# When the top-k rounds of an attention layer run on VectorE: one tile's rounds spread over other score units

## The reference

```python
s_h = jnp.einsum('bthd,bsd->bths', qib, ki)
s_idx = jnp.einsum('bths,bth->bts', jax.nn.relu(s_h), wib)
s_idx = jnp.where(causal[None], s_idx, -jnp.inf)
_, sel = lax.top_k(s_idx, topk)              # topk = 128 of at most 512 keys
...
logits = jnp.where(valid[:, None], logits, -jnp.inf)
p = jax.nn.softmax(logits, axis=-1)
return jnp.einsum('bhtk,btkhd->bthd', p, vg.astype(jnp.float32))
```

## Time and profile before

| | us |
|---|---|
| median of 3 runs | 781.57 |
| lowest, highest | 778.15, 786.66 |
| profiled execution, whole | 778.69 |
| its span, first to last instruction | 776.9 |
| TensorE busy (matmul) | 715.9 |
| VectorE busy | 462.6 |
| ScalarE busy | 338.2 |
| GpSimd busy | 265.9 |
| mean granted TensorE clock, share of full speed | 0.974 |

### The profile page before, as it was taken

How to read it: one execution, slowest core, us unless ns; L and a number is a source line. 1 busy time by engine, 2 the same in 40 slices (tenths; PEclk the granted TensorE clock), 3 DMA queues, 4 the chain that set the end, 5 groups by cost and what they waited for, 6 DMA issues and landing times.

```text
span 776.9 us, 9937 instructions
## 1 busy us (share of the span) xinstructions
PE 715.9 (92%) x3584; PEld 569.2 (73%) x3584; DVE 462.6 (60%) x831; ACT 338.2 (44%) x508; POOL 265.9 (34%) x209
## 2 busy tenths in 40 slices
PE   0898999999788879889799999999999999999998
PEld 0786877787574546678698888888878887888886
DVE  4858788886899787878553665764455445000005
ACT  3534246836522644532366455554544554111110
POOL 2003798409902200000022444344334434433440
PEclk9989999999979989899989999999999999999999
DMA  8941231160274643773811313322331332232202
GB/s 305 384 122 37 101 105 58 68 188 17 30 76 72 199 155 110 270 271 108 298 55 31 128 60 106 108 84 78 108 108 61 102 108 87 76 109 109 85 23 108
DMA packets 63017, 91.46 MB, mean 118 GB/s; under 512 B 11947, under 2 KB 41411, under 8 KB 62916
## 3 DMA queue, kind: packets, MB, share of 16 engines
q1 hardware_dynamic: 59456, 89.44, 35.8%
q10 hardware_dynamic: 3523, 1.54, 0.7%
HBM read 86.28 MB, written 4.69 MB: 117 GB/s over the span
## 4 chain that ended last, share of the span: by engine, by line
PE 80%; DVE 11%; ACT 5%; issue 3%; DMA 1%; ACTq 0%; SPq 0%; DVEq 0%
PE bank L1577 23%; PE bank L1579 23%; PE bank L1578 23%; PE bank L1582 3%; PE bank L1608 1%; DVE arena L1286 1%; PE bank L1920 1%; DVE stat L1283 1%; DMA xh<-in_x 1%; PE bank L1587 1%; PE bank L1808 1%; DVE arena L1151 1%; DVE stat L1070 1%; PE bank L1915 1%; PE bank L1788 1%
## 5 line engine op out<-in xcount | busy, mean ns | idle before, releaser
L482 POOL TENSOR_TENSOR w_lo<-w_raw,w_hi 128x2048 fp32r<-128x2048 f32 x34 | 156.8, 4612 | 387.0 <-ACT w_hi L676 192.8
L1577 PE MATMUL bank<-act_hi,w_hi 128*128 128x512 f32 (+2 forms) x384 | 148.1, 386 | 4.8 <-DVE act_lo L1514 3.2
L1578 PE MATMUL bank<-act_lo,w_hi 128*128 128x512 f32 (+2 forms) x384 | 146.9, 383 | 0.0
L1579 PE MATMUL bank<-act_hi,w_lo 128*128 128x512 f32 (+2 forms) x384 | 146.8, 382 | 0.0
L1577 PE MATMUL bank<-w_hi,act_hi 128*128 128x512 f32 x240 | 101.2, 422 | 2.1 <-DVE act_lo L1180 2.1
L1578 PE MATMUL bank<-w_lo,act_hi 128*128 128x512 f32 x240 | 96.8, 403 | 0.0
L1579 PE MATMUL bank<-w_hi,act_lo 128*128 128x512 f32 x240 | 96.7, 403 | 0.0
L676 ACT ACTIVATE w_hi<-w_raw 128x2048 fp32r<-128x2048 f32 x26 | 49.7, 1913 | 88.0 <-PE bank L1579 87.4
L1577 PEld LDWEIGHTS bank<-act_hi,w_hi 128*128 128x128 f32 x384 | 73.2, 191 | 19.8 <-issue 3.9
L1578 PEld LDWEIGHTS bank<-act_lo,w_hi 128*128 128x128 f32 x384 | 73.3, 191 | 14.3 <-issue 0.2
L1579 PEld LDWEIGHTS bank<-act_hi,w_lo 128*128 128x128 f32 x384 | 73.2, 191 | 14.3
(11 more groups left out here) (303 smaller groups left out, 1192.9 us busy)
## 6 DMA issues: line engine op xcount, KB each, us to landing
w_raw<-in_w_up SPq DMA_DIRECT2D x44, 512.0 KB, 4.5
arena<-in_w_ada SPq DMA_DIRECT2D x6, 2048.0 KB, 15.3
w_raw<-in_w_down SPq DMA_DIRECT2D x22, 512.0 KB, 4.1
w_raw<-in_w_in SPq DMA_DIRECT2D x10, 1024.0 KB, 5.0
arena<-in_w_ada SPq DMA_DIRECT2D x8, 1024.0 KB, 6.5
xh<-in_x SPq DMA_DIRECT2D x8, 512.0 KB, 8.4
w_raw<-in_w_out SPq DMA_DIRECT2D x4, 1024.0 KB, 12.5
s_mem<-in_w_ada SPq DMA_DIRECT2D x4, 1024.0 KB, 7.1
```

The lines of the kernel that those rows point to most:

```text
L482: nc.gpsimd.tensor_tensor(w_lo[:, slot, 0:width], w_raw[:, slot, 0:width], w_hi[:, slot, 0:width].bitcast(F32), ALU.subtract).then_inc(S[" ...
L1577: T.matmul(dst, lhs_hi, rhs_hi, start=start, stop=False)
L1578: T.matmul(dst, lhs_hi, rhs_lo, start=False, stop=False)
L1579: return T.matmul(dst, lhs_lo, rhs_hi, start=False, stop=stop)
```

## The change

The 48 rounds stay the same, as do the three endings and their places. Only the units behind which the rounds stand differ.

```diff
-ROUNDS = {**{i: 2 for i in (*range(8), *range(16, 24))}, **{i: 4 for i in range(8, 12)}}
+ROUNDS_AHEAD = 3
+ROUNDS = {1: {0: 2, 1: 2, 2: 4, 3: 5}, 2: {4: 2, 5: 2, 6: 2, 7: 2, 8: 4, 9: 4},
+          3: {10: 1, 11: 1, 13: 1, 15: 1, 16: 2, 17: 2, 18: 2, 19: 1, 20: 1, 21: 1, 22: 2, 23: 1}}
 
 def top_k_rounds(i):
 
-    t = i // HEADS + 1
-    return ((t,),) * ROUNDS.get(i, 0), ((t,) if i < 24 and i % HEADS == 7 else ())
+    return tuple((t,) for t in ROUNDS for _ in range(ROUNDS[t].get(i, 0))), (
+        (i // HEADS + 1,) if i < 24 and i % HEADS == 7 else ())
...
+            top_k(((1,),) * ROUNDS_AHEAD, ())
             ada_at = [0]
             for i in range(0, ATT_UNITS, 2):
                 logits(i)
```

## The result

The changed kernel takes 786.0 us, the median of 12 runs (780.97 to 789.01), against 781.85 us for the kernel before (12 runs). The ratio is 1.0055, with a 95% interval of 1.0028 to 1.0081: slower by some 4 us, where 5.6 us less were forecast. The profiled execution took 780.97 us (span 779.2), 2.3 us more than the 778.69 of before, so the trace shows a little over half of the loss.

A forecast was written before the change was run, and what follows sets the result against it. TensorE was taken to bound the kernel, VectorE most of the mixer stage. Gains of 3.6 (earlier gate product) and 3.1 (its clock), less 1.1 (`y`'s clock), gave 781.6 - 5.6 = 776.0 us, range 770.5 to 782.5.

The forecast's parts named there:

- Steps 1 and 2: Three rounds fill VectorE's 2.95 us wait at cost 0; thirteen over units 0 to 3 make unit 4's scores 0.7 late.
- Step 3: Units 4 to 7: eight rounds of tile 2 replace eight of tile 1; VectorE now 0.95 us late.
- Step 5: Units 10 and 11: two tile 3 rounds replace eight of tile 2; after waits for ScalarE's copies, first scan 2.1 us earlier.
- Step 1's sentence: GpSimd computing beside the three rounds laid ahead adds nothing to their 0.985 us each.
- Step 6: Units 12 to 15: `y` for half 0 starts 0.6 us earlier; unit 16's scores 0.9 late, hidden in VectorE's 4.57 wait.
- The clock terms: TensorE: first gate product at full clock, gain 3.1 us; `y` for half 0 partly at the lower level, loss 1.1.
- the rival with the slow gate product: First gate product stays at the lower clock: gain only 2.5 us, 779.1 us; chance 0.18.
- The rival named Slower: All of `y` for half 0 at the lower clock, gate product slow: 2.3 us slower, 783.9, or 789.8; chance 0.06.
- Step 7: Units 18 to 23: fewer tile 3 rounds bring second `g_lo` 3.03 us earlier, first gate product released 3.6 us earlier.

The follow-up runs named there:

- e1: Changed kernel with `add_d` for half 0 moved behind unit 10's scores and round, where GpSimd is done: 782.06 us, ratio 0.9969 to the kernel before.
- e6: Kernel before with one round of tile 3 moved from unit 16 to unit 15, ahead of tile 2's ending: 787.73 us, ratio 1.0074.
- e3: Changed kernel with five `keep_busy` instead of one ahead of unit 16's scores: 781.53 us, ratio 1.0010 to the kernel before.
- e4: Changed kernel with `add_d` for half 0 moved, tile 2's ending moved and five `keep_busy` ahead of unit 16's scores: 780.28 us, ratio 0.9968.
- e11: e4 with four `keep_busy` ahead of unit 12's scores as well: 777.77 us, ratio 0.9947 to the kernel before.
- e2: Changed kernel with tile 2's ending moved from unit 15 to unit 11, away from GpSimd: 782.02 us, ratio 0.9999 to the kernel before.
- e9: Changed kernel with `add_d` for half 0 moved as in e1 and GpSimd's first subtraction waiting for tile 2's mask: 779.4 us, ratio 0.9962.
- e10: Changed kernel with `add_d` for half 0 behind unit 10's scores and tile 2's ending behind unit 11: 778.83 us, ratio 0.9960.
- e5: Kernel before with one round of tile 2 moved from unit 9 to unit 8, ahead of `add_d`: 785.04 us, ratio 1.0055.
- e12: Kernel before with four `keep_busy` calls in TensorE's wait of 3.16 us ahead of the first gate product: 782.73 us, ratio 1.0001.

## Why the prediction was wrong

**Steps 1 and 2** held: no wait before 175 but 0.24, unit 4's scores at 17.13 for 17.11.

**Step 3** was 0.75 short: unit 8's scores at 29.70 for 28.94. The ending of tile 1, for which the step allowed the 0.6 of before, took 1.44 under GpSimd's instruction.

**Step 5** is the step that failed. It looked for the price of `add_d` in what it waits for, ScalarE's copies, and these waits came out about as said (1.36 + 1.47 + 1.30 = 4.1 us before `add_d` for half 1 and the scan, where 3 to 4 were forecast). But it left `add_d` for half 0, which had its data, at 0.35 us, without a look at what GpSimd would have in flight. It took 2.65. With step 3's 0.75, unit 10 is 3.03 later than forecast, the scan 3.33, and `y` for half 0 3.41: the forecast gain of 0.6 turned into a loss of 2.8.

**Step 1's sentence** "no contention shows" was true of the rounds and is where the error sits: I had tested MAX8 and MATCH_REPLACE8 beside GpSimd, found them unchanged, and let that stand for all of VectorE. Forms behave differently, and the page of the kernel before had the row that says so: costliest groups first, then VectorE and GpSimd in the MLP stage.

```profile
L1542 DVE TENSOR_TENSOR up<-conv 128x512 f32<-128x512 f32 x22 | 42.4, 1967 | 19.8 <-ACT conv L1034 19.7
```

```profile
428.61 3.68 DVE L1542 TENSOR_TENSOR up<-conv 128x512 f32<-128x512 f32 x2
432.49 1.29 DVE L1546 TENSOR_TENSOR ff_lo<-up,ff_hi 128x512 fp32r<-128x512 f32 x2 [0.20 <-ACT ff_hi L1038]
```

```profile
426.51 4.63 POOL L482 TENSOR_TENSOR w_lo<-w_raw,w_hi 128x2048 fp32r<-128x2048 f32 x1 [2.63 <-ACT w_hi L1017]
```

The pair at line 1542 takes 3.68 us, of the same 128x512 as the pair at line 1546, which takes 1.29: the pair at 1542 begins inside GpSimd's instruction (426.51 to 431.14), the other behind it. All 22 instructions of line 1542 are in eleven such pairs: the first of each takes 3.1 to 3.3 us and ends behind a GpSimd instruction, the second takes 0.68 beside an idle GpSimd. A mean of 1967 ns for an operation that takes 0.68 alone was to be asked about. The Trainium skill (SBUF — State Buffer, section Who interferes with whom) has the rule as well: VectorE and GpSimd share one pair of SBUF ports, and whoever issues first holds it for the whole instruction. A VectorE instruction with two SBUF inputs meets a GpSimd instruction that reads SBUF, and so can a copy or `tensor_scalar` in a two-port mode; one with at most one SBUF input outside those modes doesn't. The traces agree: 0.21 us becomes up to 2.05 for one instruction of the first kind, 0.36 becomes 3.62 for the second (no trace shows in which mode the ending ran), and nothing changes for MAX8 and for the scores, whose other input is in PSUM.

**Step 6.** "Hidden" was right for its 0.9 us and, barely, for what came: unit 16's scores were 7.6 late (3.62 - 0.36 of it by the ending), and in the profiled execution TensorE had no wait at 257.31, since it was late itself. The cover is thin, though: in the same place TensorE waits 0.38 us in e1's trace and 1.95 in e6's. No rival priced it.

**The clock terms.** In the trace of the changed kernel the gate product came out as forecast in place and size (3.12 us won, 3.1 forecast), but by luck: the reason given, TensorE's wait of 3.16 us in front of it, does not decide it. Without that wait the product ran at the full clock in the traces of the changed kernel, e3, e4 and e11, and at the lower level, as in the rival with the slow gate product, in those of e1, e2, e9 and e10. In e10:

```profile
286.39 2.07 PE L1840 MATMUL bank<-arena,ones 1*128 1x512 f32 x2
294.69 1.12 PE L1840 MATMUL bank<-arena,ones 1*128 1x512 f32 x2
...
286.39:294.69 8.30, 8.30 (x26) 5.48 (x24) 2.52 (x7) 0.84 (x2) 0.00 (x0) 0.56 0.06 22
```

The loss on `y` came at its place, behind a TensorE wait of over 4 us (4.78), but was mis-sized: 2.57 instead of 1.1, since the lower level covered 6 us of `y` (granted clock 0.50 up to 247.2) and not 2.5. Its cause is only half told by that wait: with it filled, in e3, 1.48 of the 2.57 stayed. And a second lower stretch, behind `y` for half 0, cost 1.38 that no term had. The rival named Slower, which forecast 783.9, is not what happened either: it had `y` lose over 3.6 us and the gate product slow.

**Step 7** was exact: from the first to the second `g_lo` 9.41 us for 12.45, 3.04 less where 3.03 was forecast, and it is 9.4 in e1, e9 and e10 too.

**The sum by the second gate product** (forecast -5.6, measured +0.59): 3.41 up to `y` for half 0, of which 0.75 and 2.3 are read off at the collisions and 0.4 is not traced further, 1.47 and 1.38 from the clock, together 6.26, which leaves 0.07. Behind that product the changed kernel loses another 1.2 up to the output projection and 1.45 in the rest, and starts the stage 0.95 earlier: +0.59 + 1.2 + 1.45 - 0.95 = 2.3, the difference of the spans.

**What stays open.** The medians differ by 4.2 us and the two traces by 2.3. The changed kernel's three slowest runs (788.7 to 789.0 us) have a mean granted clock of 0.955, the other nine (781.0 to 786.8) 0.959 to 0.967; only one execution is traced, so where the others lose the clock can't be read. The single edits e1, e2 and e3 bring back 0.86, 0.56 and 0.45% and together 0.87; that a part of each lies in where the clock falls afterwards is argued, not shown.

What is shown is that with both collisions gone and all the rest of the change in place (e9, e10) the kernel is faster than before by 0.4%, 3 us, where the prediction said 5.6. Where these 3 us come from the traces don't show. Step 7's 3.0 us are there, but the 0.6 of step 6 is not (`y` for half 0 starts at 66.18 in e9 and 66.36 in e10, 66.25 before), and with the gate product and parts of `y` at the lower level the second gate product comes later than before, at 120.90 and 121.62 for 117.40. Both traced executions (781.7 and 782.3 us) are slower than the medians of their kernels. In the traces of e4 and e11, where the gate product ran at the full clock, it comes at 115.28 and 112.89, against 111.8 in the forecast.

## What to carry to other kernels

When an instruction is moved on VectorE, look at every small one behind it: which form it has, and what GpSimd has in flight at its new time. If it has two SBUF inputs, or is a `tensor_scalar` from SBUF to SBUF like the ending here, its price is up to the rest of GpSimd's instruction. Count this for each instruction by itself, since two in a row can pay twice. Before anything else, compare each group's mean on the page with the duration of the same shape elsewhere: a mean three times too high is a wait that the idle column doesn't show. Where such an instruction gates TensorE, let GpSimd's bulk work wait for it, as in e9, or put it where GpSimd is idle.

## What the runs showed of the hardware

- The wait is booked as busy time of the waiting instruction, not as idle time with a releaser: one instruction on 32x64 elements at up to 2.05 us for 0.21, 128x384 at 3.62 for 0.36, 128x512 at 3.1 to 3.3 for 0.68.
- A waiting VectorE instruction ends 0.07 to 0.22 us behind the GpSimd instruction that was in flight when it began (in the MLP stage, at 128x512, 0.55 behind it), also where GpSimd's next follows directly (201.57, 208.17 and 254.43 in the changed kernel, 209.10 in e5). The second of two VectorE instructions then meets that next one and waits again; where GpSimd left a gap of 0.08 us (207.01 to 207.09 in the kernel before) it did not.
- Eight `keep_busy` matmuls in TensorE's wait ahead of the gate product took the lower stretch on themselves (granted clock 0.51 from 281.4 to 284.8), and the product ran at the full 2.4 GHz (e12). Ten of them ahead of unit 16's scores did not keep `y` for half 0 there: 9.17 us in e3, 10.24 in e4, 9.14 in e11, for 7.69. In all three a wait of 1.3 us and one of 1.6 stood between the filler and `y`.
- Nearly the same waits of TensorE (1.78 and 1.54 us, the others under 0.8) stood ahead of the gate product in the changed kernel, where it ran at 2.4 GHz, and in e10, where the granted clock over it was 0.56.
